# Half of the output projection moved into the last mLSTM head's chunk loop

## The reference, cut to what matters

```python
y = jnp.concatenate([y_hy, y_ml, y_rg], axis=-1)         # 2048 x 1024
x = x + mod[:, :, 2] * (y @ p['w_out'])                   # output projection, gated residual
x = x + mod[:, :, 5] * sq_relu_mlp(modulate(x, norm2_g, mod, 3), mlp_w1, mlp_w2)
```

## Time and profile before

| | |
|---|---|
| median of 3 runs | 2757.82 us (2756.74 to 2758.73) |
| the profiled execution's own time | 2759.13 us |
| its span | 2757.3 us |
| PE busy | 2550.4 us, 92% of the span |
| DVE busy | 1710.4 us, 62% |
| ACT busy | 1009.5 us, 37% |
| POOL busy | 456.4 us, 17% |
| last head's chunk loop | about 1240 to 1305 us of the span |
| output projection stage | 1305 to 1490 us |
| entry into the MLP, until PE is steady | 1490 to 1517 us |
| MLP | from 1517 us to the end |

### The profile page before, as it was taken

How to read it: one execution, slowest core, us unless ns; L and a number is a source line. 1 busy time by engine, 2 the same in 40 slices (tenths; PEclk the granted TensorE clock), 3 DMA queues, 4 the chain that set the end, 5 groups by cost and what they waited for, 6 DMA issues and landing times.

```text
span 2757.3 us, 37657 instructions
## 1 busy us (share of the span) xinstructions
PE 2550.4 (92%) x14948; PEld 1394.5 (51%) x14948; DVE 1710.4 (62%) x2843; ACT 1009.5 (37%) x1960; POOL 456.4 (17%) x357
## 2 busy tenths in 40 slices
PE   6788999997779897996998999999999999999998
PEld 2445656543575876864454444444444444444443
DVE  5751545877975565648347877878776444544445
ACT  2744444457342332324455423333233321222122
POOL 0400003700105526104223111011110000000000
PEclk8899999998989898999999999999999999999999
DMA  7311112200102122013331534343347222122212
GB/s 211 101 51 42 35 43 73 74 27 1 27 9 71 55 33 62 26 40 83 71 130 65 186 104 145 117 143 118 131 141 245 79 84 84 43 84 84 84 58 62
DMA packets 138424, 229.12 MB, mean 83 GB/s; under 512 B 15080, under 2 KB 76008, under 8 KB 133640
## 3 DMA queue, kind: packets, MB, share of 16 engines
q1 hardware_dynamic: 136520, 220.41, 24.7%
q0 software_dynamic: 1728, 6.29, 0.7%
HBM read 163.60 MB, written 62.92 MB: 82 GB/s over the span
## 4 chain that ended last, share of the span: by engine, by line
PE 51%; DVE 2%; POOL 1%; issue 1%; ACT 0%; DVEq 0%; POOLq 0%; ACTq 0%
PE pb L2343 24%; PE pb L2283 21%; PE pb L2263 6%; POOL arena L1345 1%; PE pb L2252 1%; POOL MS L1337 0%; DVE arena L1808 0%; DVE arena L1816 0%; DVE arena L1887 0%; DVE arena L1769 0%; DVE arena L1898 0%; DVE arena L1637 0%; DVE arena L1873 0%; DVE arena L1765 0%; ACT arena L1200 0%
## 5 line engine op out<-in xcount | busy, mean ns | idle before, releaser
L2343 PE MATMUL pb<-arena 128*128 128x512 f16 x3072 | 667.9, 379 | 0.0
L2283 PE MATMUL pb<-arena 128*128 128x512 f16 (+2 forms) x2736 | 590.1, 377 | 8.8 <-DVE arena L1816 4.9
L2343 PEld LDWEIGHTS pb<-arena 128*128 128x128 f16 x3072 | 300.6, 98 | 362.4
L1898 DVE SCALAR_TENSOR_TENSOR arena<-pb,arena 128x512 f32<-128x512 f32 x512 | 352.4, 690 | 185.6 <-PE pb L2343 184.2
L307 PE MATMUL pb<-arena 128*128 128x512 f16 (+1 forms) x1992 | 424.2, 374 | 18.5 <-ACT arena L1086 7.7
L2283 PEld LDWEIGHTS pb<-arena 128*128 128x128 f16 x2736 | 267.3, 99 | 326.4 <-DVE arena L1816 6.1
L307 PEld LDWEIGHTS pb<-arena 128*128 128x128 f16 x1992 | 195.6, 99 | 245.5 <-issue 20.8
L1873 DVE TENSOR_TENSOR arena<-arena,pb 128x512 f32<-128x512 f32 x224 | 149.1, 683 | 251.2 <-PE pb L2283 251.2
L1229 ACT ACTIVATE arena<-arena 128x512 f32<-128x512 f32 x256 | 160.3, 626 | 172.2 <-DVE arena L1873 167.9
L1229 ACT ACTIVATE arena<-pb 128x512 f32<-128x512 f32 x32 | 19.0, 595 | 511.2 <-PE pb L2283 510.4
L1808 DVE SCALAR_TENSOR_TENSOR arena<-arena 128x512 f16<-128x512 f32 (+1 forms) x144 | 172.5, 1217 | 13.7 <-ACT arena L1177 13.4
(11 more groups left out here) (307 smaller groups left out, 3199.1 us busy)
## 6 DMA issues: line engine op xcount, KB each, us to landing
w1x<-arena SPq DMA_DIRECT2D x16, 1792.0 KB, 8.6
arena<-w1x SPq DMA_DIRECT2D x16, 1792.0 KB, 9.3
arena<-in_x SPq DMA_DIRECT2D x128, 128.0 KB, 4.1
arena<-in_mlp_w SPq DMA_DIRECT2D x64, 256.0 KB, 3.7
arena<-in_mlp_w SPq DMA_DIRECT2D x16, 1024.0 KB, 6.3
w2x<-arena SPq DMA_DIRECT2D x16, 1024.0 KB, 8.4
arena<-w2x SPq DMA_DIRECT2D x16, 1024.0 KB, 4.9
arena<-in_w_in SPq DMA_DIRECT2D x26, 512.0 KB, 4.0
```

The costliest lines, as they stand in the source:

```text
L1898: dve.scalar_tensor_tensor(xs, pb[:, 4 + n % 4, :], 1.0 / (WS * AS), xs, ALU.mult, ALU.add).then_inc(S("acc"), 1)
L2283: mm = pe.matmul(pb[:, (7 * g + j) % 4, c], W1P[g % 2][WDEST[a]][0][:, ws, P * k:P * k + P], token_op(b, L // 2, c)[:, k, hs, :], start=(k ...
L2343: mm = pe.matmul(pb[:, 4 + n % 4, :], ACTP[sl][:, 2 * f + th, hs, P * tt:P * tt + P], W2P[sl][:, f, ws, BLK * dh:BLK * dh + BLK], start=(f ...
```

## The change

The projection of the first eight token tiles (tile m = chunk m, m = 0 to 7), 16 halves of 24 matmuls, moves from the stage into the last head's loop. In iterations 4 to 15 one half is done, twelve matmuls ahead of `ktr` and `ytr` and twelve behind them; in iterations 16 and 17 two halves are done, of which the second is split like that. All of them write PSUM bank 1, so a half waits until the residual of the half before it has been added. DVE adds the residual of each half at the end of its iteration. The pieces of `w_out` are handled column half by column half (`wo_piece`), two pieces an iteration from the start of the loop and six ahead of it on POOL, so that the first column half is ready in iteration 4 and the second in iteration 8. Squares of the eight tiles are taken by ACT in the loop (`loop_square`, a whole tile at once). x is loaded in three parts: six tiles before the second half of `w_out`, two when all 16 pieces are done, eight when the loop has ended.

In the stage, PE does the other eight tiles (t = 8 to 15) in eight steps (s = t - 8), and each step carries a whole pair: the transposes of tiles 2s and 2s + 1, their modulation, and the pair's sums and splits one step later. Half of the modulation goes from ACT to DVE (`affine_hi`). At the first step DVE waits for all eight late tiles of x.

```diff
+        LOOP_MM = {n: [(n - 4, 0)] if n < 8 else [(n - 8, 1)] for n in range(4, 12)}
+        LOOP_MM.update({12: [(4, 0)], 13: [(4, 1)], 14: [(5, 0)], 15: [(5, 1)], 16: [(6, 0), (6, 1)], 17: [(7, 0), (7, 1)]})
+        LOOP_SQ = {9: (0,), 10: (1,), 11: (2,), 12: (3,), 14: (4,), 16: (5,), 17: (6,), 18: (7,)}
```

SP:

```diff
+            sp.wait_ge(S("p_mm"), units_to_end(JOBS[-1]))
+            for g in range(4):
+                load_wo(g)
+            for i in NEAR:
                 load_tokens(sp, x1(i), ORD[i], S("x_in3"))
+            for g in range(4, 8):
+                sp.wait_ge(S("wo_lo"), 2 * (g - 3))
+                load_wo(g)
             sp.wait_ge(S("wo_lo"), 2 * KT)
+            for i in LATE:
+                load_tokens(sp, x1(i), ORD[i], S("x_in2"))
             sp.wait_ge(S("m_ylo"), NT * NH)
-            for i in range(EARLY, NT):
+            for i in range(HALF, NT):
                 load_tokens(sp, x1(i), ORD[i], S("x_in2"))
```

ACT, in the loop:

```diff
-                    if h == NH - 1 and n >= 3:
-                        wo_hi(n - 3)
+                    if h == NH - 1 and n < 8:
+                        for i in (2 * n, 2 * n + 1):
+                            wo_hi(i)
+                    if h == NH - 1:
+                        for m in LOOP_SQ.get(n, ()):
+                            loop_square(m)
```

ACT, in the stage:

```diff
+            for s in range(HALF):
+                t = HALF + s
+                if s >= 1:
+                    for i in (1, 2, 3):
+                        o_hi(s - 1, i)
                     act.wait_ge(S("h_sq"), N5 + t)
                 square(t, 0)
+                affine(2 * s)
+                if s < HALF - 1:
+                    affine(2 * s + 1)
+                if s >= 1:
+                    for i in (4, 5, 6, 7):
+                        o_hi(s - 1, i)
+                if s == HALF - 1:
                     for i in (1, 2):
                         w_hi(0, i)
                 square(t, 1).then_inc(S("h_sq"), 1)
```

POOL, in the loop and in the stage:

```diff
+                if cn == NT * (NH - 1):
+                    for i in range(6):
+                        wo_gate(i)
...
+                if 0 <= c < 5:
                     pool.wait_ge(S("m_yo"), cn + 1)
+                    for i in (6 + 2 * c, 7 + 2 * c):
+                        wo_gate(i)
...
+            for s in range(1, HALF + 1):
+                t = HALF + s - 1
                 pool.wait_ge(S("h_ms"), N5 + t + 1)
                 pool.tensor_tensor(rst2[:, t:t + 1], ssq2[:, t:t + 1], mhalf[:], ALU.pow).then_inc(S("h_rs"), 1)
+                o_add(s - 1, (1, 2, 3, 4))
```

DVE, in the loop:

```diff
-                    if h == NH - 1 and n >= 4:
-                        wo_lo(n - 4)
+                    if h == NH - 1 and 1 <= n < 9:
+                        for i in (2 * n - 2, 2 * n - 1):
+                            wo_lo(i)
...
+                    if h == NH - 1:
+                        for e, (m, dh) in enumerate(LOOP_MM.get(n, ())):
+                            if n == 4:
+                                dve.wait_ge(S("x_in3"), TOK0 + 16 * CPT * len(NEAR))
+                            if (m, dh) == (6, 0):
+                                dve.wait_ge(S("x_in2"), TOK0 + 16 * CPT * len(LATE))
+                            residual(home(m), dh, 1, loop_count(n, e + 1))
```

DVE, in the stage (`residual` is L1826 and waits for `o_mm`, `mean` is L1839 and waits for `h_sq`, `normed` is L1844, `affine_hi` modulates the upper four blocks):

```diff
+            for s in range(HALF):
+                t = HALF + s
+                normed(2 * s)
+                if s == HALF - 2:
+                    mean(t - 1)
+                if s < HALF - 1:
+                    normed(2 * s + 1)
+                if s >= 1:
+                    for i in (1, 2, 3):
+                        o_lo(s - 1, i)
+                if s == 0:
+                    dve.wait_ge(S("x_in2"), TOK0 + 16 * CPT * (len(LATE) + HALF))
+                residual(t, 0, 2 * (t % 2), 2 * t + 1)
+                if 1 <= s < HALF - 2:
+                    mean(t - 1)
+                affine_hi(2 * s)
+                if s < HALF - 1:
+                    affine_hi(2 * s + 1)
+                if s >= 1:
+                    for i in (4, 5, 6, 7):
+                        o_lo(s - 1, i)
+                if s == HALF - 1:
+                    w_add(0, (1, 2, 3))
+                    for i in (1, 2):
+                        w_lo(0, i)
+                residual(t, 1, 2 * (t % 2) + 1, 2 * t + 2)
+                if s == HALF - 2:
+                    mean(t)
```

PE, in the loop, behind the outputs of chunk n:

```diff
+                def out_half(m, dh, count, ks):
+                    if ks[0] == 0:
+                        pe.wait_ge(S("wo_lo"), KT * (dh + 1))
+                        pe.wait_ge(S("m_ylo"), NT * (NH - 1) + m + 1)
+                        if count >= 2:
+                            pe.wait_ge(S("o_x1"), count - 1)
...
+                    for e, (m, dh) in enumerate(parts):
+                        out_half(m, dh, loop_count(n, e + 1), range(KT) if e + 1 < len(parts) else range(KT // 2))
                     if n < NT - 2:
                         ktr(i0 + 20 + n, n + 1)
                     if n >= 2:
                         ytr(n - 2)
+                    if parts:
+                        m, dh = parts[-1]
+                        out_half(m, dh, loop_count(n, len(parts)), range(KT // 2, KT))
```

PE, in the stage:

```diff
+            for t in range(HALF, NT):
+                c0, s = P * ORD[t], t - HALF
                 for dh in range(2):
+                    pe.wait_ge(S("o_x1"), max(2 * t + dh - 3, 2 * HALF))
...
+                    if dh == 0:
+                        token_transposes(2 * s)
+                        if s < HALF - 1:
+                            token_transposes(2 * s + 1)
```

More of the change, by code:

```diff
@@ L1634, in wo_lo, with residual @@
             def wo_lo(i):
-                k, c = wo_half(i)
+                k, c, src = wo_piece(i)
                 dve.wait_ge(S("wo_hi"), i + 1)
-                dve.scalar_tensor_tensor(wop[:, k, 1, c], wos[k % 4][:, c], WS, wop[:, k, 0, c], ALU.mult, ALU.subtract
+                dve.scalar_tensor_tensor(wop[:, k, 1, c], src, WS, wop[:, k, 0, c], ALU.mult, ALU.subtract
                                          ).then_inc(S("wo_lo"), 1)
+            def residual(t, dh, bank, count):
+                c = slice(BLK * dh, BLK * dh + BLK)
+                dve.wait_ge(S("o_mm"), count)
+                dve.scalar_tensor_tensor(x1(t)[:, c], pb[:, bank, :], 1 / WS, x1(t)[:, c], ALU.mult, ALU.add
+                                         ).then_inc(S("o_x1"), 1)
             for h in range(NH):
@@ L1816, in o_lo, with mean @@
                 dve.tensor_tensor(dst[:, :, 1, :], o_source(p, op), dst[:, :, 0, :], ALU.subtract).then_inc(S("s_lo"), 1)
-            dve.wait_ge(S("x_in3"), TOK0 + 16 * CPT * EARLY)
-            for t in range(NT):
-                xt = x1(t)
-                for dh in range(2):
-                    c = slice(BLK * dh, BLK * dh + BLK)
-                    dve.wait_ge(S("o_mm"), 2 * t + dh + 1)
-                    if t == EARLY and dh == 0:
-                        dve.wait_ge(S("x_in2"), TOK0 + 16 * CPT * (NT - EARLY))
-                    dve.scalar_tensor_tensor(xt[:, c], pb[:, 2 * (t % 2) + dh, :], 1 / WS, xt[:, c], ALU.mult, ALU.add
-                                             ).then_inc(S("o_x1"), 1)
-                    if dh:
-                        continue
-                    if t >= 3 and t % 2:
-                        for i in range(4, 8):
-                            o_lo((t - 3) // 2, i)
-                    if t == NT - 2:
-                        w_add(0, (1, 2, 3))
-                    if t == NT - 2:
-                        for i in (1, 2):
-                            w_lo(0, i)
+            def mean(t):
                 dve.wait_ge(S("h_sq"), N5 + t + 1)
@@ new lines, in affine_hi @@
+            def affine_hi(u):
+                dve.wait_ge(S("h_tr"), N5 + u + 1)
+                if u >= 4:
+                    dve.wait_ge(S("s_lo"), 7 * (u // 2 - 1))
+                    dve.wait_ge(S("s_add"), 4 * (u // 2 - 1))
+                for k in range(KT // 2, KT):
+                    ins = dve.tensor_scalar(hf2[u % 4][:, k, :], pb[:, 5 + 2 * (u % 2), P * (k - 4):P * (k - 4) + P],
+                                            affA[:, 2, k:k + 1], affB[:, 2, k:k + 1], ALU.mult, ALU.add)
+                ins.then_inc(S("h_aff_hi"), 1)
@@ new lines, in _ @@
+            dve.wait_ge(S("h_sq"), N5 + HALF)
+            dve.tensor_scalar(ssq2[:, 0:HALF], ssq2[:, 0:HALF], EPS, None, ALU.add).then_inc(S("h_ms"), HALF)
+            for s in range(HALF):
[26 more added lines that the diff above has]
+                    mean(t)
@@ L1848, in _ @@
+            mean(NT - 1)
+            normed(NT - 1)
             for i in (3, 4, 5, 6):
                 w_lo(0, i)
+            affine_hi(NT - 1)
             for i in range(1, 8):
@@ L2219, in ytr @@
                     pe.transpose(pb[:, 0, 0:P], YO, ident[:]).then_inc(S("m_yt"), 1)
+                def out_half(m, dh, count, ks):
[4 more added lines that the diff above has]
+                            pe.wait_ge(S("o_x1"), count - 1)
+                    for k in ks:
```

(5 more changed lines are left out.)

105 lines of the change are left out of this document (50 added, 55 removed).

## The result

| | before | after |
|---|---|---|
| median | 2757.28 us (4 runs) | 2781.34 us (4 runs, 2774.24 to 2781.98) |
| ratio | | 1.0081, 95% interval 1.0064 to 1.0099 |
| own time of the profiled execution | 2759.13 us | 2780.95 us |
| its span | 2757.3 us | 2779.2 us |
| PE busy | 2550.4 us | 2550.9 us |

The change makes the kernel slower by 24 us in the median, and the interval of the ratio lies wholly above 1. PE does the same work; the three differences sum to +21.8, the difference of the two spans (21.9), so the segments hold all of it. Runs of one kernel differ by up to 15 us, and the start of the last head's loop differs between traces by up to 11. A segment that no edit touches is steadier: from the loop's first residual to S it is 123.74 to 123.78 us in the four traces that share it.

A forecast was written before the change was run, and what follows sets the result against it. The prediction took PE to bound the output-projection stage and DVE the loop ahead of it. Loop +81.9, stage -68.1 and MLP entry +0.4 gave +14.2 us on 2757.8, so 2772.0 us, range 2752 to 2786.

The forecast's parts named there:

- rival 1: Stage stays bound by PE, x in time and turn under 12.1 us: 2755.5 us, no change; chance 0.18.
- rival 2: Stage: both norms of a turn fall beside a sum, turn 14.4, five add 7.5 us: about 2780; chance 0.20.
- The products in the loop: Loop iterations 4 to 14: period 8.89 us, half tile paid in full, eleven periods add 56.7 us.
- rival 3: Loop: hand-over to DVE is covered, period falls to 1.97 + 5.18 us: 2748.5 us, faster; chance 0.10.
- Weights ahead: Loop's start: earlier pieces of the output weights make three iterations take 13.0 instead of 10.52 us, +2.5 us.
- The drain: Loop's end, from chunk 15's outputs to the stage: 32.0 us instead of 11.09, +20.9 us.
- loop part: Last head's loop: weight pieces, products, low-part waits and drain together add 81.9 us.
- The late x: Stage's start: DVE's first residual waits for all eight late tiles, landing about 18 us after the stage starts.
- The turn: Stage, first to fifth step: a pair's chain takes 12.9 us, longer than PE's 12.1; five turns make 64.5.
- Steps 5 to 7: Stage's end: last two steps start sums early; tile 15's transposes come 24.7 us after step 6's first residual.
- The stage: Output projection behind the loop: start to tile 15's transposes takes 116.5 us instead of 184.6, -68.1 us.
- Clock: Stage's start: PE arrives busy and saves 1.8 us, which the wait for x takes; loop idling priced at nothing.

The follow-up runs named there:

- run 7: Changed kernel with each half tile in the loop making only 2 of its 24 products, waits, banks and residuals kept: 2723.52 us (one run).
- run 1: Changed kernel with DVE's residual of a loop half tile moved into the next iteration, behind the weights: 2758.35 us, ratio 1.0002.
- run 2: Changed kernel with DVE waiting for late x tile 8 in step 0, tile 9 in step 1, the other six in step 2: 2770.36 us.
- run 6: Changed kernel with run 1, run 2 and run 3 combined, two PSUM banks in iterations 16 and 17, earlier means, POOL sums delayed except last pair: 2741.71 us.
- run 3: Changed kernel with POOL's sums of pairs 5 and 6 waiting for DVE's third low part of the pair: 2774.02 us, ratio 1.006.
- run 4: Changed kernel with PE's transposes of tile 15 placed ahead of the first 24 MLP products: 2781.87 us, ratio 1.0081.

## Why the prediction was right, and where it was off

The forecast was slower, 2772.0 in 2752 to 2786; the kernel took 2781.34. The causes were the ones named: halves paid in full, one wait for all of x, and a pair's chain longer than PE's turn. The range of 34 us holds rivals 1 and 2 too, so the parts say more than the total. Point by point:

- **The products in the loop** were forecast at a period of 8.89 and took 8.88. Run 7 bears out the reason (a half is paid in full) and run 1 the rest: the 1.73 that rival 3 would have saved is 1.75. That rival needed the order on DVE that the change does not have.
- **Weights ahead** +2.5: the first four periods grew from 13.19 to 16.44, +3.3. The periods of iterations 4 and 8, whose products need the eighth and the sixteenth low part, were 1.72 and 0.97 longer than 8.88, 2.7 in place of 1.8. In iteration 4 PE shows no idle time ahead of the products: its granted clock was 0.60 (1255 to 1258), and they start 0.06 behind the low part (1258.24). Their first twelve took 3.10 in place of 2.75. The drain with its own iteration grew by 26.5 us, against 26.05, because a hand-over costs 1.04 to 1.10 and not 0.9. The loop itself started 0.8 earlier in this trace. The loop part came to **+83.0, forecast +81.9**.
- **The late x**: 20.4 after S, not 18 (+2.4). I had scaled the busy time of 44 loads to 32 (0.55 us each). A wait ends with the landing of the last load, and by the landings in the trace of the kernel before the 32nd came at S + 19.2; more on this below. That it would be waited for as a whole was right, and run 2 shows that this wait costs 11 us.
- **The turn** of the pair's chain was 12.46, not 12.9 (four turns, -1.8), and the first began 7.2 after x, not 7.5 (-0.3). It was longer than PE's 12.1 nevertheless: rival 1 falls, and run 6 shows what it takes to get there.
- **Steps 5 to 7, the step that failed.** I wrote "In the forecast the norms run after the sums, so only POOL's longer times count", and followed the last two steps instruction by instruction "at the same durations". In steps 6 and 7, whose sums start early, norm and low parts fall beside the sums. From step 5's residual to step 6's it is 16.85 against 14.7 (0.3 and 1.5 of store among it; the store did cost 1.11), and from there to T15 30.5 against 24.7. Together +8.0 us; run 3 takes 5.1 of it back by delaying POOL. This is rival 2's mechanism in a place where I had not put it: not a norm in each of five turns, but norms and low parts in the last two. The other 2.9 are the MLP's first products ahead of T15 (its norm ends at 1509.9). They are mostly no loss: the entry behind T15 shrank by 1.5 where +0.4 was forecast, and without them, in run 4, the MLP starts 1.4 earlier, 0.5 of it because of x.
- **The stage** came to S + 124.9, forecast S + 116.5: **-59.7 in place of -68.1**. With the loop's +1.1 and the entry's -1.9 the sum is +21.8 in place of +14.2. The medians differ by 2.3 more than that, which is within the spread of the runs.
- **Clock**: the first 24 products of the stage took 5.35 (rather than the share of 17.30 for 72), as said.

The rule of the Trainium skill (GPSIMD Engine Reference, Key points) weighed in the prediction, contention of POOL with DVE's two-input instructions on SBUF, is borne out by run 3: three low parts 4.03 beside the sums and 1.89 without. The norm, which has one tensor input, slows as well (1.75 and 0.75). By that rule, applied also to the last two steps, the forecast would have been some 5 us higher.

## What to carry to other kernels

In this case PE's free time in a loop bound by hand-overs was free only when the filler ran inside the wait: put the filler's follow-up on the other engine (here one residual) behind the instruction that PE waits for next, or the filler is paid in full. A wait for a whole group of transfers ahead of the first use costs the group's time even when the bandwidth is there. When a reordering packs the element-wise work of VectorE and GpSimd side by side, price each with the other running, in every step, and look whether starting the helper later ends the pair sooner.

## What the runs showed of the hardware that was not expected

**Contention is selective.** Beside POOL's sums three low parts (two f32 operands in SBUF) went from 1.90 to 4.03 us and the norm (one operand, 128x1024 f32) from 0.75 to 1.75, while instructions that read PSUM kept their times. The residual at 1482.42 takes 0.68 beside POOL's sum of 1482.04 (1.59 us), as it does with POOL idle at 1415.71. `affine_hi` takes 2.63 for eight blocks of 128x128 with POOL idle (1409.11) and 2.64 mostly beside a sum (1416.38).

**The same 32 loads of x landed after 19.9 to 23.6 us.** In the busy times by stretch of the kernel after (us, PE, PEld, DVE, ACT, POOL, granted clock, DMA share, GB/s):

```profile
1388.00:1394.00 6.00, 5.91 (x31) 3.12 (x32) 1.87 (x6) 1.02 (x2) 1.65 (x1) 1.00 0.80 208
...
1394.00:1404.00 10.00, 10.00 (x53) 5.14 (x52) 0.00 (x0) 0.00 (x0) 0.00 (x0) 1.00 1.04 232
...
1404.00:1409.00 5.00, 1.55 (x8) 0.49 (x5) 0.50 (x1) 0.00 (x0) 0.00 (x0) 1.00 0.71 130
...
1409.00:1415.00 6.00, 1.94 (x9) 1.95 (x10) 5.77 (x14) 5.68 (x15) 0.00 (x0) 0.52 0.01 1
```

The middle runs at 232 GB/s; at that rate the 4.19 MB would take 18.1 us, and the other 2.3 lie at the two ends. In the first us behind S no bytes move. The first load lands at S + 2.2, the 31st at S + 19.5 (one every 0.58 us), and the last at S + 20.4, 0.9 behind. The 130 GB/s of the third stretch is an average over full rate and, from about 1407, nearly nothing. In the other traces the last load lands 0.9 to 4.0 us behind the one before it: 4.0 in run 7, where the 31st had landed at S + 19.6, and 3.3 in the kernel before. A wait for all tiles pays this; what makes the last load so late stays open.

**The clock** fell in PE's idle time at the stage's start: granted 0.52 in the stretch 1409 to 1415 (full, 1.00, is 2.4 GHz; half is 1.2), with 7.5 us of idle PE up to 1413.06. The 16 transposes there took 3.39 us, where the 16 ahead of them in the same trace (1393.28) and those of run 6 took 1.91 with PE busy ahead. At the end the MLP's first 24 products took 6.63 after 4.60 us of idle PE. The sum had such slow work in the stage at zero. At the stage's start it cost nothing that the trace shows: `affine_hi` starts 0.67 behind the residual there (1416.38) as in step 5 (1466.24). What it cost at the end no run separates.
